# A turned strip's sixteen block moves: SyncE begins all of them, ScalarE none

## The chip, the cores and the metric

One core of one Trainium2 chip. The metric is the time of one launch on the device, in microseconds (us). TensorE (PE in the profile), VectorE (DVE), ScalarE (ACT), GpSimd (POOL) and SyncE (SP) each run their own list of instructions in order and meet at semaphores. SyncE computes nothing: it begins DMA transfers and waits.

## What is computed

One decoder layer over 256 tokens of width 2048 in float32. Cut to what matters here:

```python
h = rmsnorm(x, g_mix);  proj = h @ w_in                       # twelve parts: q, k, v, indexer, gates
out_a = dsa_sparse_attention(...);  out_b = forgetting_attention(...)
mixed = sigmoid(gate_a) * (out_a @ w_o_a) + sigmoid(gate_b) * (out_b @ w_o_b)
x = x + mixed @ w_out
h = rmsnorm(x, g_ffn)
x = x + (silu(h @ w_ffn_gate) * (h @ w_ffn_up)) @ w_ffn_down  # 5632 wide
h = rmsnorm(x, g_ple)
x = x + sigmoid(h @ w_ple_gate) * (p @ w_ple_proj)
return rmsnorm(x, g_final)
```

## The kernel before, in words

**Weights.** All weights stream from HBM in chunks of 512 KB (two tiles of 128 rows by 512 columns, in the stages that matter here). SyncE loads a chunk into one of four slots `ws` (`load`, L279). ScalarE copies it, rounded, into `hs` (`split_high`, L416), VectorE stores the rest `ws - hs` in `ls` (`split_low`, L720), and TensorE uses both (`by_token`: L1275 with `hs`, twice, for the high and low part of the activations; L1280 with `ls`). There are four slots of each. SyncE may load chunk c when VectorE has split chunk c-4 (`slot_free`); ScalarE may split chunk c when TensorE has used chunk c-4. A chunk waits for its high split before its first matmul and for its low split before its last four.

**Stages.** From the middle of the kernel on, results are made in strips of 512 columns. A "WO" stage (four of them) takes 8 chunks of `w_o_b` and `w_o_a` and makes one strip of `mixed`. An "OUT" stage (four) takes 8 chunks of `w_out` and makes one strip of x. An FFN pair (eleven; ten of them in a loop of two per pass) takes 8 chunks of the gate and 8 of the up weights and makes one strip of `ff`. A "DOWN" stage (four) takes 22 chunks, a "PLE" stage (four) takes 9. The stages follow each other without a gap in TensorE's list.

**Turning.** TensorE leaves a strip with tokens on the partitions, and the next product needs it with columns on the partitions. VectorE transposes 32x32 blocks of the strip into `t_rows` (`turn_quads`, L989, two instructions, semaphore `turned`). Sixteen DMAs inside SBUF, 32 KB each, then move block (a, q) to block (q, a) of `t_cols` (`move_quads`, L224, semaphore `moved`). Half of them, with q even, are begun by SyncE, the other half by ScalarE. When all sixteen have landed, ScalarE and VectorE write the high and the low part of the strip (`mixed_high` L570 and `mixed_low` L994; `new_high` L598 and `new_low` L1023; `ff_hi` L646 and `ff_low` L1090). 23 strips are turned: four of `mixed`, four of x after OUT, eleven of `ff`, four of x after DOWN.

**Order.** All lists are written out by hand. In SyncE's list the moves of the strip that the last stage made stand behind the loads of the first eight chunks of the running stage; the loads of the next chunks stand behind the moves. With the chunks of a stage called c0, c1, ..., the order is: load c0 to c7, wait for `turned`, begin 8 moves, load c8 (the c0 of the next stage where a stage has eight chunks), and so on. In ScalarE's list (`split_and_move`) the other 8 moves stand between the high splits of c5 and c6, and behind c7 stands the high part of the strip, then (WO stages) two sigmoids of the gates (L581), then the high splits of c8 to c11. VectorE's list is: low splits of c4 to c7, low part of the strip, low splits of c8 to c11, then the work on the finished strip (WO: three instructions from L1008 on; OUT and DOWN: L1030) and the turn.

Most stages use the turned strips of an earlier kind of stage and have long had them. Three strips are wanted at once: the fourth strip of `mixed`, by chunk c6 of the first OUT stage; the fourth strip of x, by c6 of the first FFN pair; the fourth strip of x after DOWN, by c7 of the first PLE stage.

Of the kernel before, what the change touches and what calls it, by code (L numbers as in the profile page):

```python
# [62 lines left out]
N_WIDE = D_MODEL // WIDE  # L63
N_FFN = D_FF // WIDE
C_WO, C_OUT, C_FFN = 4 * U_WO, 4 * U_OUT, 4 * U_FFN
# [8 lines left out]
QUADS = P // QUAD  # L74
# [38 lines left out]
def hybrid_layer(nc, c_rows, x, p, positions, g_mix, w_in, b_f, w_o_a, w_o_b, w_out, g_ffn, w_ffn_gate,  # L113
# [102 lines left out]

        return t.rearrange("p k (b a n) -> p (k b) a n", b=2, a=QUADS)

    def move_quads(eng, t, odd):

        eng.wait_ge(turned, 2 * t + 2)
        for a in range(QUADS):
            for q in range(odd, QUADS, 2):
                eng.dma_start(t_cols[QUAD * q:QUAD * (q + 1), a, :, :, :],  # L224
                              t_rows[QUAD * a:QUAD * (a + 1), q, :, :, :]).then_inc(moved, 16)

# [37 lines left out]
    @block.sync  # L264
    def _(sp):

        for b in range(2):
            sp.dma_start(x_tok[:, b, :], x_rows[:, b, :]).then_inc(x_loaded[b], 16)
        for n, g in enumerate((g_mix[0], g_ffn[0], g_ple[0])):
            sp.dma_start(gain_rows[n * KT:(n + 1) * KT, :], g.rearrange("(t q) -> t q", q=P)).then_inc(gains_loaded, 16)  # L270
        sp.dma_start(bias_f[F_ROWS, :], b_f[0].rearrange("(h o) -> h o", o=1)).then_inc(bias_loaded, 16)

        def slot_free(u, j):

            sp.wait_ge(l_split, 4 * (u - 1) + j + 1)

        def load(j, src, n=CHUNK):
            parts = src.shape[1]
            sp.dma_start(ws[:, j, 0:n].rearrange("p (t n) -> p t n", t=parts), src).then_inc(w_loaded[j], 16)  # L279


        sp.wait_ge(ring_zero, SLOTS)
        for j in range(SLOTS):
            slot = ws[:, j, 0:SMALL].rearrange("p (t n) -> p t n", t=KC)
            rows = win_t[:, KC * j:KC * j + KC, :]
            for at, col, n in ((0, AT_KI, D_IDX + H_IDX), (F_ROW, AT_FB, HB)):
                sp.dma_start(slot[:, :, at:at + n], rows[:, :, col:col + n]).then_inc(w_loaded[j], 16)

        def columns(u0, units, w, col0):

            with sp.Fori(0, units) as i:
                for j in range(SLOTS):
                    slot_free(u0 + i, j)
                    load(j, w[:, KC * j:KC * j + KC, ds(col0 + i * GROUP, GROUP)])

        columns(U_QI, 4, win_t, AT_QI)
        columns(U_QB, 8, win_t, AT_QB)

        def wide_columns(u0, units, w, col0):

            with sp.Fori(0, units) as i:
                for c in range(K_CH):
                    slot_free(u0 + c // SLOTS + i * (K_CH // SLOTS), c % SLOTS)
                    load(c % SLOTS, w[:, KW * c:KW * (c + 1), ds(col0 + i * WIDE, WIDE)])

        wide_columns(U_VB, 2, win_t, AT_VB)
        wide_columns(U_GA, N_WIDE, win_t, AT_GA)
        columns(U_QA, 6, win_t, AT_QA)
        wide_columns(U_GB, N_WIDE, win_t, AT_GB)
        for i in range(N_WIDE):  # L310
            for c in range(K_CH):
                slot_free(U_WO + c // SLOTS + i * 2, c % SLOTS)
                w, t = (wob_t, woa_t)[c // SLOTS], KW * (c % SLOTS)
                load(c % SLOTS, w[:, t:t + KW, WIDE * i:WIDE * (i + 1)])
            if i > 0:
                move_quads(sp, T_MIX + i - 1, 0)

        sp.wait_ge(o_ready, FREE + HEADS)
        sp.dma_start(p_tok[:, :, :], p_rows).then_inc(p_loaded, 16)
        for i in range(N_WIDE):  # L320
            for c in range(K_CH):
                slot_free(U_OUT + c // SLOTS + i * 2, c % SLOTS)
                load(c % SLOTS, wout_t[:, KW * c:KW * (c + 1), WIDE * i:WIDE * (i + 1)])
            move_quads(sp, T_MIX + N_WIDE - 1 + i, 0)
        with sp.Fori(0, N_FFN) as i:
            for half, w in enumerate((wgate_t, wup_t)):
                for c in range(K_CH):
                    slot_free(U_FFN + 2 * half + c // SLOTS + i * 4, c % SLOTS)
                    load(c % SLOTS, w[:, KW * c:KW * (c + 1), ds(i * WIDE, WIDE)])
                if half == 0:  # L330
                    move_quads(sp, T_FF - 1 + i, 0)
        for n in range(N_WIDE):
            for c in range(FF_CH):
                at = C_DOWN + FF_CH * n + c
                slot_free(at // SLOTS, at % SLOTS)
                load(at % SLOTS, wdown_t[:, KW * c:KW * (c + 1), WIDE * n:WIDE * (n + 1)])
                if c == K_CH - 1:
                    move_quads(sp, T_PLE - 1 + n, 0)
        for n in range(N_WIDE):
            cols = slice(WIDE * n, WIDE * (n + 1))  # L340
            for c in range(PLE_CH):
                at = C_PLE + PLE_CH * n + c
                slot_free(at // SLOTS, at % SLOTS)
                load(at % SLOTS, wpp_t[:, :, cols] if c == 0 else wpg_t[:, KW * (c - 1):KW * c, cols])
                if n == 0 and c == K_CH - 1:
                    move_quads(sp, T_PLE + N_WIDE - 1, 0)

        for n in range(2):
            cols = slice(D_MODEL // 2 * n, D_MODEL // 2 * (n + 1))
            sp.wait_ge(y_ready_0, 2 * n + 2)  # L350
            sp.dma_start(out_rows[:, 0, cols], out_tok[:, 0, cols]).then_inc(out_stored, 16)
        cols = slice(WIDE * 3, D_MODEL)
        sp.wait_ge(y_ready_0, 5)
        sp.dma_start(out_rows[:, 1, cols], out_tok[:, 1, cols]).then_inc(out_stored, 16)
        sp.wait_ge(out_stored, 4 * 16)
# [50 lines left out]
    def _(act):  # L406
# [152 lines left out]
            for at in range(first, first + n):  # L559
                split_high(at // SLOTS, at % SLOTS)  # L560

        def split_and_move(first, t):

            split_chunks(first, 2)
            move_quads(act, t, 1)
            split_chunks(first + 2, 2)

        def mixed_high(n):
            act.wait_ge(moved, 16 * MOVES * (T_MIX + n + 1))
# [3 lines left out]
        for n in range(N_WIDE):  # L573
            cols = slice(WIDE * n, WIDE * (n + 1))
            if n == 0:
                split_chunks(C_WO + 4, 4)
            else:
                split_and_move(C_WO + 8 * n + 4, T_MIX + n - 1)
                mixed_high(n - 1)
            for gate in (1, 0):  # L580
                act.activation(gates[:, gate, :, cols], gates[:, gate, :, cols], ACT.Sigmoid).then_inc(gate_ready, 1)  # L581
            split_chunks(C_WO + 8 * n + 8, 4)
# [20 lines left out]
            act.activation(rms[:, stage, 0, :], sum_sq[:, stage, :], ACT.Sqrt, bias=eps[:, 0:1], scale=1.0 / D_MODEL).then_inc(rms_sqrt, 1)  # L603

        for n in range(N_WIDE):
            split_and_move(C_OUT + 8 * n + 4, T_MIX + N_WIDE - 1 + n)
            if n == 0:
                mixed_high(N_WIDE - 1)
                act.wait_ge(p_t, 1)
                act.activation(p_cols[:, :, 0:TOK], side[:, 2, :].rearrange("p (m n) -> p m n", m=2), ACT.Copy).then_inc(p_high, 1)  # L610
            else:
                squares(0, n - 1)
                new_high(0, n - 1)
            split_chunks(C_OUT + 8 * n + 8, 4)

        def ff_pair(i, step, first=False):

            u = U_FFN + 4 * step + i * 8
            c = step + i * 2
            split_high(u + 1, 0)  # L620
            split_high(u + 1, 1)
            move_quads(act, T_FF - 1 + c, 1)
            split_high(u + 1, 2)
            split_high(u + 1, 3)
            if first:
                squares(0, 3)
                new_high(0, 3)
                root(0)
            else:
                ff_hi(c - 1)  # L630
            for j in range(SLOTS):
                split_high(u + 2, j)
            if first:
                act.wait_ge(rms_ready, 1)
            for b in range(2):
                ins = act.activation(silu_g[:, b, :], acc[:, 2 + b, :], ACT.Silu, scale=rms[:, 0, 1, b:b + 1])
            ins.then_inc(ff_silu, 1)
            for j in range(SLOTS):
                split_high(u + 3, j)
            for j in range(SLOTS):  # L640
                split_high(u + 4, j)
# [10 lines left out]

        for n in range(N_WIDE):
            at = C_DOWN + FF_CH * n
            split_and_move(at + 4, T_PLE - 1 + n)
            if n == 0:
                ff_hi(N_FFN - 1)
            else:
                squares(1, n - 1)
                new_high(1, n - 1)  # L660
            split_chunks(at + 8, FF_CH - 4)
# [5 lines left out]
        for n in range(N_WIDE):  # L667
# [1 line left out]
            if n > 0:  # L669
                split_chunks(at + 4, 4)  # L670
            if n == 0:
                split_and_move(at + 4, T_PLE + N_WIDE - 1)
                squares(1, 3)
                new_high(1, 3)
                act.dma_start(g_out[:, :], g_final.partition_broadcast(P)).then_inc(g_out_loaded, 16)
# [816 lines left out]
```

## Time and profile before

| | |
|---|---|
| median of 3 runs | 1491.15 us (1489.91 to 1491.16) |
| the profiled execution | 1490.77 us |
| its span, first to last instruction | 1489.0 us |
| TensorE matmuls busy | 1459.5 us (98%) |
| ScalarE, VectorE busy | 690.6 us (46%), 884.0 us (59%) |
| DMA engines | 61.8% of their time on SyncE's queue, 2.1% on ScalarE's |
| bytes moved | 290.91 MB |

The profiled execution took 1.8 us more than its span, which lies before the first and behind the last instruction. DMA-issuing instructions are not counted as busy; in a timeline they stand under SPq and ACTq, the sequencers' own rows. A row of a timeline gives start, duration from the first to the last instruction that it merges, engine, line, operation, output and input, and the count; in brackets stands how long the engine was idle before it and what ended that.

### The profile page before, as it was taken

How to read it: one execution, taken by the hardware profiler on the slowest of the kernel's cores; microseconds unless marked ns; L12 is line 12 of the kernel's file. 1: busy time of each engine (PE TensorE's matmuls, PEld its weight loads, DVE VectorE, ACT ScalarE, POOL GpSimd, SP SyncE). 2: the span in 40 equal slices, each digit the busy share in tenths (PEclk: the TensorE clock that was granted, in tenths of full speed). 3: DMA queues.
4: the chain of work that ended last, by engine and by line, in shares of the span. 5: the costliest groups of instructions: out<-in, count | busy, mean ns of one | idle time of the engine just before them, and what ended most of it. 6: DMA issues, size and time to landing. Idle time of an engine off the chain costs nothing.

```text
span 1489.0 us, 19456 instructions
## 1 busy us (share of the span) xinstructions
PE 1459.5 (98%) x6841; PEld 1222.0 (82%) x6841; DVE 884.0 (59%) x1066; ACT 690.6 (46%) x846; POOL 49.9 (3%) x80
## 2 busy tenths in 40 slices
PE   5999999999999999999999999999999999999996
PEld 5888888888888888887888888888888888888885
DVE  6966776667655576665555555455555455554654
ACT  5644445544444455445444444444444343443544
POOL 0021001100111000000000000000000000000000
PEclk9999999999999999999999999999999999999998
DMA  6666565556655577666666666766666766666663
GB/s 193 178 204 169 160 222 170 169 170 190 183 166 167 163 236 232 211 208 214 205 209 210 202 191 205 212 207 210 205 204 184 221 204 197 210 190 209 213 215 109
DMA packets 182574, 290.91 MB, mean 195 GB/s; under 512 B 18745, under 2 KB 67825, under 8 KB 182001
## 3 DMA queue, kind: packets, MB, share of 16 engines
q1 hardware_dynamic: 172944, 281.02, 61.8%
q10 hardware_dynamic: 9568, 9.07, 2.1%
q8 instruction: 39, 0.64, 0.2%
q14 instruction: 23, 0.18, 0.0%
HBM read 275.87 MB, written 2.11 MB: 187 GB/s over the span
## 4 chain that ended last, share of the span: by engine, by line
PE 94%; DVE 3%; DMA 1%; ACT 1%; ACTq 1%; issue 0%; DVEq 0%
PE acc L1275 50%; PE acc L1280 25%; PE acc L1165 8%; PE acc L1174 4%; PE side L1275 2%; PE side L1280 1%; DVE ls L720 1%; ACTq L224 1%; DMA rope_c<-in_rope_rows 1%; PE side L1321 0%; DVE hn L775 0%; PE side L1327 0%; DMA t_cols<-t_rows 0%; ACT hs L416 0%; PE side L1335 0%
## 5 line engine op out<-in xcount | busy, mean ns | idle before, releaser
L720 DVE TENSOR_TENSOR ls<-ws,hs 128x1024 fp32r<-128x1024 f32 (+1 forms) x520 | 629.9, 1224 | 535.7 <-ACT hs L416 531.3
L416 ACT ACTIVATE hs<-ws 128x1024 fp32r<-128x1024 f32 (+1 forms) x520 | 544.1, 1056 | 717.8 <-PE acc L1280 505.0
L1275 PE MATMUL acc<-hs,xg 128*128 128x512 f32 x1648 | 407.1, 389 | 1.1 <-DVE xg L1023 1.1
L1275 PEld LDWEIGHTS acc<-hs,xg 128*128 128x128 f32 x1648 | 309.3, 188 | 65.6 <-DVE xg L1023 1.5
L1280 PE MATMUL acc<-ls,xg 128*128 128x512 f32 x824 | 220.2, 389 | 0.0
L1280 PEld LDWEIGHTS acc<-ls,xg 128*128 128x128 f32 x824 | 154.7, 188 | 32.1
L1275 PE MATMUL acc<-hs,ff 128*128 128x512 f32 x704 | 173.8, 389 | 0.0
L1275 PE MATMUL acc<-hs,hn 128*128 128x512 f32 (+1 forms) x704 | 171.9, 387 | 0.0
L1275 PEld LDWEIGHTS acc<-hs,ff 128*128 128x128 f32 x704 | 132.2, 188 | 27.4
L1275 PEld LDWEIGHTS acc<-hs,hn 128*128 128x128 f32 x704 | 127.1, 188 | 24.2
L1165 PE MATMUL acc<-hn,hs 128*128 128x512 f32 x560 | 139.2, 393 | 0.0
L1165 PEld LDWEIGHTS acc<-hn,hs 128*128 128x128 f32 x560 | 101.5, 189 | 18.9
L1280 PE MATMUL acc<-ls,ff 128*128 128x512 f32 x352 | 94.1, 389 | 0.0
L1280 PE MATMUL acc<-ls,hn 128*128 128x512 f32 (+1 forms) x352 | 90.4, 380 | 0.0
L1174 PEld LDWEIGHTS acc<-hn,ls 128*128 128x128 f32 x560 | 74.3, 191 | 5.1 <-DVE hn L775 0.7
L1280 PEld LDWEIGHTS acc<-ls,ff 128*128 128x128 f32 x352 | 66.1, 188 | 13.7
L1174 PE MATMUL acc<-hn,ls 128*128 128x256 f32 x560 | 75.9, 283 | 0.5 <-DVE hn L775 0.5
L1280 PEld LDWEIGHTS acc<-ls,hn 128*128 128x128 f32 x352 | 64.2, 188 | 13.1
L1275 PE MATMUL acc<-hs,mixed 128*128 128x512 f32 x256 | 63.5, 390 | 0.5 <-DVE mixed L994 0.5
L1275 PEld LDWEIGHTS acc<-hs,mixed 128*128 128x128 f32 x256 | 47.9, 188 | 10.9 <-DVE mixed L994 1.0
L533 ACT ACTIVATE lg<-lg,neg_max 128x128 f32<-128x128 f32 (+1 forms) x32 | 14.3, 448 | 47.0 <-DVE neg_max L935 47.0
L1280 PE MATMUL acc<-ls,mixed 128*128 128x512 f32 x128 | 34.2, 389 | 0.0
(192 smaller groups left out, 815.2 us busy)
## 6 DMA issues: line engine op xcount, KB each, us to landing
ws<-in_w_in SPq DMA_DIRECT2D x152, 512.0 KB, 3.9
ws<-in_w_ffn_gate SPq DMA_DIRECT2D x88, 512.0 KB, 4.4
ws<-in_w_ffn_up SPq DMA_DIRECT2D x88, 512.0 KB, 4.4
ws<-in_w_ffn_down SPq DMA_DIRECT2D x88, 512.0 KB, 4.3
ws<-in_w_out SPq DMA_DIRECT2D x32, 512.0 KB, 4.7
ws<-in_w_ple_gate SPq DMA_DIRECT2D x32, 512.0 KB, 3.9
ws<-in_w_o_b SPq DMA_DIRECT2D x16, 512.0 KB, 4.6
ws<-in_w_o_a SPq DMA_DIRECT2D x16, 512.0 KB, 4.6
```

The lines of the kernel that those rows point to most:

```text
L224: eng.dma_start(t_cols[QUAD * q:QUAD * (q + 1), a, :, :, :], t_rows[QUAD * a:QUAD * (a + 1), q, :, :, :]).then_inc(moved, 16)
L416: act.activation(hs[:, j, 0:n], ws[:, j, 0:n], ACT.Copy).then_inc(h_split, 1)
L533: act.activation(lg[:, cols], lg[:, cols], ACT.Exp, bias=neg_max[:, b:b + 1], accum_out=sums[:, b:b + 1]).then_inc(exp_done, 1)
L720: dve.tensor_tensor(ls[:, j, 0:n], ws[:, j, 0:n], hs[:, j, 0:n].bitcast(F32), ALU.subtract).then_inc(l_split, 1)
L1165: mm = pe.matmul(acc_of(bank + m, 2 * TOK), hs[:, j, at], src[:, k, :], start=first and q == 0, stop=last and q == len(tiles) - 1)
L1174: mm = pe.matmul(acc_of(bank + m, TOK), ls[:, j, at], src[:, k, 0:TOK], start=False, stop=False)
L1275: pe.matmul(banks[b], block_of(src, k, part, b), hs[:, slot, q * width:(q + 1) * width], start=first and q == 0 and part == 0, stop=False)
L1280: mm = pe.matmul(banks[b], block_of(src, k, 0, b), ls[:, slot, q * width:(q + 1) * width], start=False, stop=last and q == len(tiles) - 1)
```

## The change

`move_quads` loses its argument `odd` and begins all sixteen moves of a strip. SyncE calls it where it called it before. ScalarE no longer calls it: `split_and_move` is gone, and four high splits stand in its place.

```diff
-    def move_quads(eng, t, odd):
+    def move_quads(eng, t):
 
         eng.wait_ge(turned, 2 * t + 2)
         for a in range(QUADS):
-            for q in range(odd, QUADS, 2):
+            for q in range(QUADS):
                 eng.dma_start(t_cols[QUAD * q:QUAD * (q + 1), a, :, :, :],
                               t_rows[QUAD * a:QUAD * (a + 1), q, :, :, :]).then_inc(moved, 16)
@@ SyncE, at all of its six call sites @@
-                move_quads(sp, T_MIX + i - 1, 0)
+                move_quads(sp, T_MIX + i - 1)
@@ ScalarE @@
-        def split_and_move(first, t):
-
-            split_chunks(first, 2)
-            move_quads(act, t, 1)
-            split_chunks(first + 2, 2)
@@
-                split_and_move(C_WO + 8 * n + 4, T_MIX + n - 1)
+                split_chunks(C_WO + 8 * n + 4, 4)
@@ and likewise for OUT, DOWN and the first PLE stage; in ff_pair @@
-            move_quads(act, T_FF - 1 + c, 1)
```

## Rows read from the trace of the kernel before

**Rows 1.** The page's busy times: busy us, share of the span, instructions.
```profile
PE 1459.5 (98%) x6841; PEld 1222.0 (82%) x6841; DVE 884.0 (59%) x1066; ACT 690.6 (46%) x846; POOL 49.9 (3%) x80
```
**Rows 2.** Waits of TensorE from 485 us on: us in total, times, longest.
```profile
PE acc L1275 <- DVE xg L1023: 1.1, 1, 1.1
PE acc L1275 <- DVE mixed L994: 0.5, 1, 0.5
```
**Rows 3.** Waits of SyncE's sequencer, whole span: us in total, times, longest.
```profile
SPq L279 <- DVE ls L720: 984.4, 470, 8.0
```
**Rows 4.** Timeline of the second WO stage, which begins at 505.79.
```profile
505.79 1.77 PEld L1275 LDWEIGHTS acc<-hs,heads_o 128*128 128x128 f32 x8
...
508.51 1.77 PEld L1275 LDWEIGHTS acc<-hs,heads_o 128*128 128x128 f32 x8
...
513.49 5.06 SPq L224 DMA_DIRECT2D t_cols<-t_rows  x8
513.49 5.38 ACTq L224 DMA_DIRECT2D t_cols<-t_rows  x8
...
518.59 4.24 SPq L279 DMA_DIRECT2D ws<-in_w_o_b  x4
518.98 2.01 ACT L416 ACTIVATE hs<-ws 128x1024 fp32r<-128x1024 f32 x2 [6.20 <-issue]
...
521.84 1.99 ACT L581 ACTIVATE gates<-gates 128x1024 f32<-128x1024 f32 x2
```
**Rows 5.** The moves, by tile: ns min/median/max, first and last start; then their landing.
```profile
L224 SPq DMA_DIRECT2D t_cols<-t_rows x184: 512/592/1624, 513.5 to 1388.6; - x184
...
DMA to landing us min/median/max: 1.8/1.9/4.5
```
**Rows 6.** Two loads begun back to back behind moves, by line L279, and each one's landing.
```profile
L279 SPq DMA_DIRECT2D ws<-in_w_o_b x1: 584/584/584, 518.6 to 518.6; - x1
DMA to landing us min/median/max: 4.6/4.6/4.6
...
L279 SPq DMA_DIRECT2D ws<-in_w_o_b x1: 482/482/482, 519.2 to 519.2; - x1
DMA to landing us min/median/max: 5.4/5.4/5.4
```
**Rows 7.** Timeline, end of that stage: merge of the next strip, and its moves.
```profile
530.89 1.22 DVE L1008 TENSOR_TENSOR mix_b<-acc,gates 128x1024 f32<-128x1024 f32 x1
...
535.87 4.97 SPq L224 DMA_DIRECT2D t_cols<-t_rows  x8
```
**Rows 8.** Timeline of the first OUT stage: the fourth strip of `mixed`.
```profile
578.77 4.97 SPq L224 DMA_DIRECT2D t_cols<-t_rows  x8
...
586.08 1.05 ACT L570 ACTIVATE mixed<-t_cols 128x1024 fp32r<-128x1024 f32 x1
...
588.81 1.69 PEld L1275 LDWEIGHTS acc<-hs,mixed 128*128 128x128 f32 x8 [0.97 <-DVE mixed L994]
```
**Rows 9.** Timeline of the second OUT stage: new x, and its moves.
```profile
596.89 1.22 DVE L1030 TENSOR_TENSOR x_tok<-acc,x_tok 128x1024 f32<-128x1024 f32 x1
...
599.47 4.96 SPq L224 DMA_DIRECT2D t_cols<-t_rows  x8
```
**Rows 10.** Timeline of the first FFN pair: the fourth strip of x.
```profile
664.75 5.83 SPq L224 DMA_DIRECT2D t_cols<-t_rows  x8
...
675.09 1.71 ACT L598 ACTIVATE xg<-t_cols,gains 128x256 fp32r<-128x256 f32 x4 [0.20 <-DMA t_cols<-t_rows]
...
677.23 2.11 PE L1275 MATMUL acc<-hs,xg 128*128 128x512 f32 x8 [1.07 <-DVE xg L1023]
```
**Rows 11.** SyncE's timeline of the second FFN pair.
```profile
709.82 5.16 SPq L224 DMA_DIRECT2D t_cols<-t_rows  x8
715.18 14.06 SPq L279 DMA_DIRECT2D ws<-in_w_ffn_up  x8
```
**Rows 12.** SyncE's timeline, second DOWN stage.
```profile
1204.68 5.97 SPq L224 DMA_DIRECT2D t_cols<-t_rows  x8
```

More of the change, by code:

```diff
@@ L323, in _ @@
                 load(c % SLOTS, wout_t[:, KW * c:KW * (c + 1), WIDE * i:WIDE * (i + 1)])
-            move_quads(sp, T_MIX + N_WIDE - 1 + i, 0)
+            move_quads(sp, T_MIX + N_WIDE - 1 + i)
         with sp.Fori(0, N_FFN) as i:
@@ L330, in _ @@
                 if half == 0:
-                    move_quads(sp, T_FF - 1 + i, 0)
+                    move_quads(sp, T_FF - 1 + i)
         for n in range(N_WIDE):
@@ L337, in _ @@
                 if c == K_CH - 1:
-                    move_quads(sp, T_PLE - 1 + n, 0)
+                    move_quads(sp, T_PLE - 1 + n)
         for n in range(N_WIDE):
@@ L345, in _ @@
                 if n == 0 and c == K_CH - 1:
-                    move_quads(sp, T_PLE + N_WIDE - 1, 0)
+                    move_quads(sp, T_PLE + N_WIDE - 1)
         for n in range(2):
@@ L605, in _ @@
         for n in range(N_WIDE):
-            split_and_move(C_OUT + 8 * n + 4, T_MIX + N_WIDE - 1 + n)
+            split_chunks(C_OUT + 8 * n + 4, 4)
             if n == 0:
@@ L654, in _ @@
             at = C_DOWN + FF_CH * n
-            split_and_move(at + 4, T_PLE - 1 + n)
+            split_chunks(at + 4, 4)
             if n == 0:
@@ L671, in _ @@
             if n == 0:
-                split_and_move(at + 4, T_PLE + N_WIDE - 1)
+                split_chunks(at + 4, 4)
                 squares(1, 3)
```

## The prediction

> **What bounds the kernel now.** I read the busy times first: TensorE's matmuls fill 1459.5 of 1489.0 us [rows 1]. Then the list of waits from 485 us on, where all the turning happens: TensorE waits twice, for the low part of the fourth `mixed` strip and of the fourth x strip [rows 2]. Everything else there is hidden behind matmuls, so there are at most some 2.3 us to win (worked out below), and the question is how much cover the moves have. SyncE's waits say where to look: it waits 984.4 us for free slots [rows 3]. That reads as an idle engine, but it is an average. Behind `turned` stands a list without such waits, and the timelines of single stages show its length.
>
> A chunk takes TensorE 508.51 - 505.79 = 2.72 us [rows 4], so a stage of eight takes 21.76 us. I write S for a stage's start, T for the start of SyncE's moves, M for the time from T to the next load, L for the start of that load.
>
> **Part 1: ScalarE loses its moves.** In the WO stage it issues for 5.38 us, and the splits of c6 and c7 come after an idle time of 6.20 us [rows 4]. Both are wanted by TensorE later than that anyway (TensorE does not wait there, [rows 2]), so removing 23 such stretches is worth nothing by itself. What could be gained is the two waits of TensorE.
>
> **Part 2: SyncE issues sixteen.** The eight moves and the step to the load take 518.59 - 513.49 = 5.10 us [rows 4]. A move takes 592 ns in the median and 512 at least, plus the step to the next [rows 5]; eight in 4.97 us are 0.63 apart [rows 8]. Eight more cost 8 x 0.63 = 5.0 us, so M goes from 5.1 to 10.1. The trace never shows SyncE issuing moves well away from ScalarE's. Bounds: 9.0 if alone each takes the shortest 512 ns plus 0.05 for the step, and 11.1 if one stretch of slow issue is met per strip, as in two of the stages (5.83 and 5.97 us for eight, [rows 10, 12]). I take 10.1, the row of most strips.
>
> The moves themselves are quick: 1.9 us to landing [rows 5]. The last of sixteen starts at T + 9.5 and lands at T + 11.4. In the x strips this costs little, because ScalarE's last moves used to land behind the next weight load: the high part began at 675.09 - 664.75 = T + 10.3 [rows 10].
>
> The Trainium skill (DMA: Bandwidth & Descriptors, section "Issuing engines are not separate DMA queues") says that issuing from several engines saves only the sequencers' time, "which is usually small relative to the DMA itself". Here eight issues take 5.0 us and one transfer 1.9, so I hold it not to be small; by the rule the sum below would be zero (the first rival).
>
> **Part 3: what is queued behind the moves on SyncE.** The load of c8. Its landing takes 4.6 us with another load right behind it [rows 6]; split and steps add 1.16 (1.06 for the instruction, about 0.05 before and behind it). So TensorE can have c8 at L + 5.8, and wants it at S + 21.76. Per kind of stage:
> - WO: T = S + 7.7 (513.49 - 505.79, [rows 4]). Before: 7.7 + 5.1 + 5.8 = 18.6, hidden. Now 7.7 + 10.1 + 5.8 = 23.6: late by **1.8**. ScalarE's own list is no later: strip at T + 11.4, its high part 1.05 [rows 8], two sigmoids 1.99 [rows 4] make T + 14.4, and c8 lands at T + 14.7.
> - OUT: T = S + 5.3 (L1030 one chunk after the stage's start, then 599.47 - 596.89 = 2.58, [rows 9]). 5.3 + 10.1 + 5.8 = 21.2: hidden by 0.6.
> - FFN pair: T is 5.45 after its start, and the step to the load is 715.18 - 709.82 = 5.36 [rows 11], so M = 10.4: 21.65, hidden by 0.1. Eight more chunks follow, in which the lists catch up.
> - DOWN: like OUT with eight moves of 5.97 [rows 12], M = 11.1: 22.2, late by 0.4, in three stages; 22 chunks let it catch up. The PLE strip goes like OUT and is hidden.
>
> **Part 4: late loads make the next strip late.** With c8 to c11 all waiting behind the moves, four loads go out together. Two begun 0.6 us apart land 1.4 us apart (518.6 + 4.6 and 519.2 + 5.4, [rows 6]), so c11 lands at L + 8.8 and its low split ends at L + 11.2. VectorE's merge of the finished strip stands behind that split. The trace shows this already: in the next stage the merge begins at 530.89 and T is 535.87, 4.98 later [rows 7], which is S + 8.3 and not 7.7. So from a WO stage T' = L + 11.2 + 4.95, and L' = T' + 10.1. Stage to stage that is 11.2 + 4.95 + 10.1 = 26.25 us against 21.76: **+4.5 for each further stage of this kind**, and T sits at S + 10.4. From an OUT stage it is 11.2 + 2.6 + 10.1 = 23.9: +2.1, T at S + 8.0.
>
> **The sum**, in order:
> - WO stages two to four: 1.8, 4.5, 5.1 (the last has the load of `p_tok`, 0.6, in the queue too): 11.4.
> - First OUT stage, fourth `mixed` strip. T = S + 10.4, strip landed + 11.4, low part complete 588.81 - 586.08 = 2.73 after the high part's start [rows 8]: S + 24.5. TensorE wants it at S + 6 x 2.72 + 0.55 for transposes in between = S + 16.9, so it waits 7.6, against 588.81 - 587.94 = 0.9 before: +6.7. This long wait lets the loads catch up.
> - OUT stages two to four: the second 0 with T = S + 5.3 (21.2), the third 1.5 (T = S + 7.4), the fourth 2.1: 3.6.
> - First FFN pair, fourth x strip: T = S + 8.0, landed + 11.4, first tiles + 2.14 (677.23 - 675.09, [rows 10]): S + 21.5. Wanted at S + 16.3: waits 5.2, against 1.45 before (the pair starts at 659.45, so wanted at 675.77): +3.8.
> - FFN 0; DOWN 3 x 0.4 = 1.2; PLE 0.
> Together 11.4 + 6.7 + 3.6 + 3.8 + 1.2 = 26.7 us. The span becomes 1515.7, the execution 1517.5. The profiled execution stood 0.4 under the median; I forecast **1517.5 us** (+1.8%).
>
> By the bounds of M alone: with 9.0 the same recurrence gives 0.7 + 3.4 + 4.0 + 5.6 + 0.3 + 2.7 = 16.7, so 1507.5. If loads in a burst land 1.95 and not 1.4 us apart, 37 us, 1528.
>
> **Rivals.**
> - *No change*, the case on the other side. The sequencers share what writes the descriptors, and a queue alone issues faster than beside another. For: issues take 512 ns at first and 592 in the median [rows 5]. Against: 512 is still a floor seen with a queue just begun. It decides at M of 6.9, 0.43 us a move: then T + M + 5.8 stays under 21.76 even with T at S + 9.0, and only the `mixed` strip costs about 1. Time 1491 to 1493. Chance 0.07. The skill's rule points here.
> - *Faster*: only the two waits of TensorE could go, 0.9 + 1.45 = 2.3 us, if in addition the strips landed sooner: 1489. Chance 0.02.
> - *Late loads but no feedback*: the four loads land early enough that T keeps its place. Then three WO stages 1.8 each and 0.6, the `mixed` strip 7.7 + 11.4 + 2.7 - 17.7 = 4.1, the x strip 5.3 + 11.4 + 2.1 - 17.8 = 1.0, DOWN 1.2: 12.3 us, 1503. Against it stands the 8.3 of [rows 7]. Chance 0.2.
> - *Slow issue in every strip*: M = 11.1, and the FFN pairs lose their cover, 5.45 + 11.4 + 5.8 - 21.76 = 0.9 in each of eleven. The recurrence gives 2.8 + 5.5 + 6.1 + 7.7 + 6.6 + 4.7 outside the FFN, 10 in it and 1.2 in DOWN: 44.6 us, 1535. Chance 0.14.
> - The forecast, with M between 9.0 and 10.5 and the spread of the burst: 1507 to 1528. Chance 0.57.
>
> **How the numbers follow.** The range leaves out no change and faster (0.09) and what lies above the slow issue; it reaches from under the case without feedback to the slow issue: 1500 to 1536. About 3 us (0.2%) is what a measurement of this kernel can tell from no change: slower 0.92, same 0.06, faster 0.02.
>
> **What would show it.** In the profile after: SyncE's rows of sixteen moves, with about 10.0 us from T to the last one's end (right for part 2 between 9.0 and 11); no ACTq row of L224, and splits of c6 and c7 on time; waits of TensorE's L1275 at the first chunk of WO stages on ScalarE's L416 and through it on DMA `ws`, of 1.8, 4.5 and 5.1 us; T at S + 10.4 in the third and fourth WO stage; a wait of over 7 us on L994 and over 5 on L1023; next to no waits between 720 and 1160 us. The prediction is wrong if SyncE's moves stand under 0.45 us apart, or if T keeps to S + 7.7 in WO stages. The FFN's cover of 0.1 us is the thinnest: if a landing there takes 5.0 instead of 4.6, eleven waits of 0.3 appear.

## The result and the profile after

The changed kernel takes **1522.16 us** (median; 1521.39 to 1525.15) against 1491.16: a ratio of 1.0214, 95% interval 1.0202 to 1.0226, or 31 us. I had forecast 1517.5 and slower. The profiled execution has a span of 1519.6 us, 30.6 more than before.

The page's busy times and its DMA queues (packets, MB, share of the 16 engines):

```profile
PE 1468.0 (97%) x6841; PEld 1226.7 (81%) x6841; DVE 888.1 (58%) x1066; ACT 696.4 (46%) x846; POOL 50.0 (3%) x80
...
q1 hardware_dynamic: 181776, 287.06, 61.3%
q10 hardware_dynamic: 736, 3.03, 0.5%
```

Against [rows 1], TensorE did the same 6841 matmuls in 8.5 us more busy time. The same bytes moved; ScalarE's queue (q10) has lost its moves to SyncE's (q1). So there is no more work anywhere, only a different order.

SyncE's timeline, which answers to [rows 4], [rows 7] and [rows 8]:

```profile
513.57 11.10 SPq L224 DMA_DIRECT2D t_cols<-t_rows  x16
524.71 2.12 SPq L279 DMA_DIRECT2D ws<-in_w_o_b  x4
...
540.50 10.02 SPq L224 DMA_DIRECT2D t_cols<-t_rows  x16
550.56 2.12 SPq L279 DMA_DIRECT2D ws<-in_w_o_b  x4
...
566.02 10.02 SPq L224 DMA_DIRECT2D t_cols<-t_rows  x16
...
593.89 10.01 SPq L224 DMA_DIRECT2D t_cols<-t_rows  x16
```

Sixteen moves take 10.0 us (11.1 the first time), and behind each of the first two blocks four weight loads go out at once, in 2.12 us. The first of them, begun at 524.71, lands in 4.6 us, as one did before [rows 6]: it is late because it is begun late, not because it is carried more slowly. The second block begins 10.0 us after its stage's start at 530.5, the third 10.0 after 556.0; before, these two blocks began 8.3 [rows 7] and 7.8 us (at 557.07) after their stages' starts.

What delayed the second block stands in VectorE's timeline:

```profile
530.41 5.19 DVE L714 TENSOR_TENSOR ls<-ws,hs 128x1024 fp32r<-128x1024 f32 x4 [2.16 <-ACT hs L416]
535.52 1.22 DVE L1002 TENSOR_TENSOR mix_b<-acc,gates 128x1024 f32<-128x1024 f32 x1
...
539.16 1.30 DVE L983 STREAM_TRANSPOSE t_rows<-mix_b 128x512 f32<-128x512 f32 x2
```

The low splits of the four late loads stand ahead of the merge (L1002, which was L1008). They end at 535.60, 10.9 us after L = 524.71, the merge follows at once, and the turn ends at 540.46, just ahead of the moves at 540.50.

All of TensorE's waits up to the second FFN pair, from its timeline (the bracket is the idle time and what ended it; the lines of TensorE and VectorE are 6 lower than before, L1269 for L1275, while L224, L279 and L416 have kept theirs):

```profile
530.52 2.06 PE L1269 MATMUL acc<-hs,heads_o 128*128 128x512 f32 x8 [2.50 <-ACT hs L416]
...
556.01 2.90 PE L1269 MATMUL acc<-hs,heads_o 128*128 128x512 f32 x8 [3.48 <-ACT hs L416]
...
582.66 2.08 PE L1269 MATMUL acc<-hs,mixed 128*128 128x512 f32 x8 [2.99 <-ACT hs L416]
607.53 3.78 PE L1269 MATMUL acc<-hs,mixed 128*128 128x512 f32 x8 [7.75 <-DVE mixed L988]
...
659.60 2.09 PE L1269 MATMUL acc<-hs,mixed 128*128 128x512 f32 x8 [0.91 <-ACT hs L416]
683.14 2.08 PE L1269 MATMUL acc<-hs,xg 128*128 128x512 f32 x8 [1.50 <-ACT hs L416]
...
704.73 3.78 PE L1269 MATMUL acc<-hs,xg 128*128 128x512 f32 x8 [4.98 <-DVE xg L1017]
```

Where [rows 2] had two waits there are seven, all ending between 530 and 705 us. Five are for a high split whose load was late, two for a strip. Note the second column: eight matmuls take 1.98 us in a running stage, 2.1 after most of the waits, but 2.90 and 3.78 after the longest. The windows say why (window; length, PE busy; granted clock; DMA share, GB/s):

```profile
558.00:560.00 2.00, 2.00 (x7) 0.50 0.94 250
...
607.50:609.50 2.00, 1.97 (x5) 0.50 1.05 405
609.50:611.50 2.00, 2.00 (x6) 0.50 0.97 374
...
613.50:615.50 2.00, 2.00 (x11) 1.00 0.83 294
```

The granted clock stood at 0.50, that is 1.2 instead of 2.4 GHz, for some 4 us of matmuls after TensorE had stood idle for 7.75 us, and came back to 1.00.

I count lateness from one chunk's start to the next, less 2.72 us, which is a little more than the idle time. Late chunks: 2.85, 3.84, 3.34, 8.12, 1.26, 1.85, 5.37, together 26.6, and 0.4 in one DOWN stage; less the 2.35 of before, 24.7. The chunks right behind three of the waits took 4.01, 4.53 and 4.86 us instead of 2.72, and two more were a little long: 6.0 us for the clock. Together 30.7 of 30.6 us.

### The profile page after: what moved, and what is told of

It reads as the page before. It is cut to its first block, busy times and chain, and to the rows that moved or that the text cites. A ratio compares the mean times of both kernels' runs of the same rounds, so it can differ in the third digit from the quotient of the medians.

```text
span 1519.6 us, 19446 instructions
## 1 busy us (share of the span) xinstructions
PE 1468.0 (97%) x6841; PEld 1226.7 (81%) x6841; DVE 888.1 (58%) x1066; ACT 696.4 (46%) x846; POOL 50.0 (3%) x80
## 3 DMA queue, kind: packets, MB, share of 16 engines
HBM read 275.87 MB, written 2.11 MB: 183 GB/s over the span
## 4 chain that ended last, share of the span: by engine, by line
PE 84%; SPq 6%; DVE 4%; DMA 4%; ACT 1%; issue 1%; DVEq 0%; ACTq 0%
PE acc L1269 45%; PE acc L1274 22%; PE acc L1159 8%; SPq L224 5%; PE acc L1168 4%; DMA ws<-in_w_out 1%; PE side L1269 1%; DMA ws<-in_w_o_b 1%; DVE ls L714 1%; DVE t_rows L983 1%; ACT hs L416 1%; DMA rope_c<-in_rope_rows 1%; SPq L279 1%; PE side L1274 0%; DMA ws<-in_w_ffn_gate 0%
## 5 line engine op out<-in xcount | busy, mean ns | idle before, releaser
L416 ACT ACTIVATE hs<-ws 128x1024 fp32r<-128x1024 f32 (+1 forms) x520 | 548.1, 1057 | 627.5 <-PE acc L1274 421.4
L1269 PE MATMUL acc<-hs,xg 128*128 128x512 f32 x1648 | 409.2, 391 | 6.5 <-DVE xg L1017 5.0
L1269 PEld LDWEIGHTS acc<-hs,xg 128*128 128x128 f32 x1648 | 310.6, 189 | 72.0 <-DVE xg L1017 5.4
L1269 PE MATMUL acc<-hs,ff 128*128 128x512 f32 x704 | 173.9, 389 | 0.0
L1269 PE MATMUL acc<-hs,hn 128*128 128x512 f32 (+1 forms) x704 | 171.9, 387 | 0.0
L1269 PEld LDWEIGHTS acc<-hs,ff 128*128 128x128 f32 x704 | 132.1, 188 | 27.8 <-issue 0.4
L1269 PEld LDWEIGHTS acc<-hs,hn 128*128 128x128 f32 x704 | 127.1, 188 | 24.2
L1269 PE MATMUL acc<-hs,mixed 128*128 128x512 f32 x256 | 65.4, 399 | 11.6 <-DVE mixed L988 7.7
L1269 PEld LDWEIGHTS acc<-hs,mixed 128*128 128x128 f32 x256 | 48.8, 192 | 23.0 <-DVE mixed L988 8.2
L1084 DVE TENSOR_TENSOR ff<-t_cols,ff 128x1024 f32 (+1 forms) x11 | 13.5, 1225 | 50.5 <-ACT ff L640 50.5
L1017 DVE SCALAR_TENSOR_TENSOR xg<-t_cols,gains,xg 128x128 fp32r<-128x128 f32 x64 | 17.5, 346 | 41.2 <-ACT xg L593 41.2
```

The lines of the kernel that those rows point to most:

```text
L416: act.activation(hs[:, j, 0:n], ws[:, j, 0:n], ACT.Copy).then_inc(h_split, 1)
L1017: ins = dve.scalar_tensor_tensor(in_quads(xg[:, 1, k:k + 1, :])[:, b], by_tile(t_cols)[:, 2 * m + b], gain, in_quads(xg[:, 0, k:k + 1, :]. ...
L1084: dve.tensor_tensor(in_quads(ff[:, 1, ds(c * 4, 4), :]), by_tile(t_cols), in_quads(ff[:, 0, ds(c * 4, 4), :].bitcast(F32)), ALU.subtract). ...
L1269: pe.matmul(banks[b], block_of(src, k, part, b), hs[:, slot, q * width:(q + 1) * width], start=first and q == 0 and part == 0, stop=False)
```

## The experiments

All times are medians, beside the kernel before on the same chip: 1490.58 us for the first four, 1490.77 for the next four, 1490.69 for the last four. Line numbers shift from kernel to kernel. In most, TensorE's product with `hs` stands at L1280 and the one with `ls` at L1285 (L1275 and L1280 before), the moves at L227, ScalarE's split at L421.

**Where does it cost? Only the FFN's eleven strips.**

```diff
 SyncE, in the FFN loop
-                    move_quads(sp, T_FF - 1 + i, 0)
+                    move_quads(sp, T_FF - 1 + i, 0, ALL)
 ScalarE, in ff_pair
-            move_quads(act, T_FF - 1 + c, 1)
+            move_quads(act, T_FF - 1 + c, 1, [])
```

> SyncE begins all sixteen moves of the eleven strips that are moved during FFN pairs (the fourth x strip and ten of ff); all other strips as before. By my theory the loads behind the moves still come in time there (turned 5.45 us after a pair's start, 10.4 to the load, 5.8 to the split: 21.65 of 21.76), so only the x strip costs: it is complete 1.0 us later than before. Expected +0.5 to +1.5 us, 1492. Rival, that each strip costs its share wherever it is (30.6 us / 23 = 1.3): 11 x 1.3 = +14.6 us, 1506. Rival, that the FFN's cover of 0.1 us is too thin: +3 to +5 us.

Measured 1493.33 us (ratio 1.002, 1.001 to 1.003): +2.8. The timeline of TensorE's weight loads shows the wait for the fourth x strip, and there is no other in the FFN:

```profile
678.56 2.38 PEld L1280 LDWEIGHTS acc<-hs,xg 128*128 128x128 f32 x8 [2.81 <-DVE xg L1028]
```

The ten strips of `ff` cost nothing; the cover of 0.1 us held. The x strip made its chunk 1.3 us later than before (2.77 against 1.45), and the chunk behind took 4.18 us, 1.5 too long, with the granted clock at 0.50. In this profiled execution half of the 3.0 us is the clock, for which I had allowed nothing. The ten executions fall into two groups, five from 1492.07 to 1492.91 (four of them within 0.1 us, +1.5, the upper end of my range) and five from 1493.75 to 1495.50. That the clock falls in the one group and not in the other would fit; only one execution was profiled, so it is not shown. A cost by share is refuted.

**Only the three strips of the WO stages.** Same edit at the WO call sites.

> SyncE begins all sixteen moves of the three strips moved during WO stages; the others as before. By my theory: first late load 1.8 to 2.9 us, then by feedback (the next strip is turned 10 us instead of 7.7 after its stage's start) 4 and 3.3, the fourth mixed strip is turned late too and its wait grows by 2 to 2.5, and one wait of over 3.4 us costs another 1.5 us at half the TensorE clock: +12 to +14 us, 1504. Rival without feedback: 3 x 1.8 + 0.6 = +6 us, 1497. Rival by share: 3 x 1.3 = +4 us.

Measured 1505.23 us (1.0104, 1.0087 to 1.012): +14.7, a little over my +12 to +14; its profiled span is 13.5 over. Late chunks of 3.0, 2.6 and 4.7 us, 2.3 for the mixed strip, and 3.0 of clock. I had expected 4 and then 3.3 us for the second and third: here the slow chunks came behind the first wait, the stage was longer by 1.5 us, and the second chunk was less late for it. Three strips of 23 make nearly half of the loss, and the rival without feedback (+6) is refuted.

**One strip only, the fourth of mixed.** The same edit for `i == 0` of the OUT loop.

> SyncE begins all sixteen moves of one strip only, the fourth strip of mixed, which TensorE wants at once. By my theory it is complete at S + 7.7 + 11.4 + 2.7 = S + 21.8 where TensorE wants it at S + 16.9: a wait of 4.5 to 4.9 us against 0.9 before, +4. After a wait of this length the granted clock should stand at half for some 3 to 4 us, as after the waits of 3.8, 8.1 and 5.4 us in the changed kernel, which costs 1.6 to 2.7 more: +5.6 to +6.5 us, 1497. Rival, that the clock has nothing to do with the wait: +4.0 us, 1495. Rival by share: +1.3.

Measured 1496.38 us (1.0045, 1.0029 to 1.0062), and 1495.96 in a second set: +5.3 to +5.8. The chunk was 5.04 us late and the next one took 4.52, 1.8 too long. The rival without the clock (+4.0) is refuted.

**ScalarE's relief alone.** SyncE's calls stay, ScalarE's are gone, `MOVES` is 8, and the consumers read `t_rows`. Half of the moves are left out, so the strips are not turned rightly; the time still bounds what ScalarE's relief can be worth.

> Part 1 alone, with work left out: SyncE begins its eight moves as before, ScalarE's eight are left out altogether and the consumers read the unmoved strip, so half of the moves' work is missing and the strips are not turned rightly. By my theory ScalarE's freed 5.3 us per strip are worth nothing but the two waits of TensorE of 0.9 and 1.45 us, which vanish since the strips are complete at T + 7: 1488.5 to 1489.5 us, -2.3. Rival, that ScalarE's issuing was a cost of its own: clearly under 1485 us.

Measured 1488.73 us (0.9989, 0.998 to 0.9999): -1.9. TensorE has no wait from 480 us on. The relief is worth no more than that, and it is the two waits of [rows 2].

**Half the dose.** `ALL[:12]` on SyncE, `ALL[12:]` on ScalarE, in every strip.

> Half the dose in all 23 strips: SyncE begins twelve moves, ScalarE four. M, the time from the turn to the next load, should be 7.6 us. By my theory 7.7 + 7.6 + 5.8 = 21.1 still hides in the first WO stage, and only the feedback of the late burst bites afterwards: waits of about 0.9, 2.2 and 4.3 us, nothing in OUT, FFN and DOWN: +6.7 us including the clock, 1497.5. Rival, that the cost is in proportion to the moves given to SyncE: half of 31 us, 1506.5. Rival of a threshold without feedback: no more than +2, 1493.

Measured 1500.04 us (1.0066, 1.0049 to 1.0083): +9.3, nearer to 1497.5 than to 1506.5, and not to 1493. This run sets the feedback apart from the late load itself. SyncE's timeline, then the start of two WO stages in TensorE's weight loads:

```profile
513.53 8.35 SPq L227 DMA_DIRECT2D t_cols<-t_rows  x12
...
537.45 7.49 SPq L227 DMA_DIRECT2D t_cols<-t_rows  x12
```
```profile
527.60 1.77 PEld L1280 LDWEIGHTS acc<-hs,heads_o 128*128 128x128 f32 x8
...
551.13 1.68 PEld L1280 LDWEIGHTS acc<-hs,heads_o 128*128 128x128 f32 x8 [1.82 <-issue]
```

The stage at 527.60 begins without any wait. But its four loads had gone out in a burst, from 521.93 on in 2.11 us, and the next moves begin at 537.45, 9.85 us after the stage's start instead of 8.3 [rows 7]. The stage after it is late by 1.8 although it has fewer us of moves in front of its load than the one that was on time. The next is late by 2.4.

**A load between the moves.** In the WO stages and the first three OUT stages: `ALL[:8]`, the next stage's first load, `ALL[8:]`.

> As the changed kernel, but in WO and OUT stages SyncE begins eight moves, then the next stage's first load, then the other eight. By my theory that load is only one of two paths that are nearly equally late: ScalarE's split of that chunk stands behind the strip's high part and two sigmoids and can't begin before T + 15. So WO stages still wait 2.1 to 3.6 us, the mixed strip 6.5, the x strip 4.8: 1513 to 1517, 5 to 9 us faster than the changed kernel. Rival, that this load's place in SyncE's queue is the whole matter: no waits in WO and OUT, only the two strips late: 1500 to 1502.

Measured 1518.41 us (1.0189, 1.0172 to 1.0206), 3.8 us below the changed kernel (3.4 when each is taken against its own kernel before): the theory's side, 1.4 us outside my numbers. The late chunks in WO are 2.2, 3.6 and 2.0 us, so the place of this one load is not the whole matter. With the load in time, ScalarE's own list is the later path: at the first of them the strip's high part begins at 525.85, two sigmoids follow, and the split of the stage's first chunk comes only at 528.71, without any wait for its load. My error was in the strips, the mixed one above all: 8.5 us late where I had 6.5, its moves beginning 10.9 us after the stage's start. I did not follow that up.

**The mirror image.** `[]` on SyncE, `ALL` on ScalarE, everywhere.

> The mirror image: ScalarE begins all sixteen moves, SyncE none. SyncE's loads are then never late and there is no feedback, but the high splits of c6 and c7 stand behind ten us of issuing: by my theory waits of 2.6 us in each of three WO stages, about 0.8 in every other stage that turns a strip, 5 to 6 for the two strips wanted at once and 3 for the third: +36 to +42 us, 1528 to 1533. Rival, that it is all the same which queue begins the moves: 1522. Rival, that only a late weight load hurts: under 1500.

Measured 1541.13 us (1.0342, 1.0325 to 1.0359): +50. Right in kind, not in size. From ScalarE's timeline of an OUT stage:

```profile
619.46 11.46 ACTq L227 DMA_DIRECT2D t_cols<-t_rows  x16
631.02 2.01 ACT L421 ACTIVATE hs<-ws 128x1024 fp32r<-128x1024 f32 x2 [10.53 <-PE acc L1285]
```

The splits of c6 and c7 stand behind the moves as expected, but the block took 11.5 us here and not 10.1, and the chunk was 2.3 us late where I had 0.8; the FFN pairs were late by 1.0 each and not 0.8. Net of the waits of before, late chunks make some 43 of the 50 us and slow chunks behind them some 7, a term that I had left out. ScalarE is the worse of the two for this, since it has a split due in every stage.

**The merge earlier.** In the changed kernel, VectorE's WO stage:

```diff
-            split_chunks(C_WO + 8 * n + 8, 4)
+            split_chunks(C_WO + 8 * n + 8, 2)
             ...
             turn_quads(mix_b, 0)
+            split_chunks(C_WO + 8 * n + 10, 2)
```

> As the changed kernel, but in WO stages VectorE merges and turns the finished strip behind the low split of c9 instead of c11. It tests the feedback (a late burst of loads delays the next turn). By my theory T in the third and fourth WO stage moves from S + 10 to S + 7.5, the waits for the late first load there fall from 3.8 and 3.3 to about 1.5 with some 1.4 new for the low split of c10, and the mixed strip's wait falls from 8.1 to about 5.5: 3 to 6 us faster than the changed kernel, 1516 to 1519. Rival without feedback, that each load is late by its sixteen moves alone: T and the first waits unchanged, and the new waits add to them: 1522 or more.

Measured 1521.46 us (1.0207, 1.019 to 1.0224): no gain that can be told. T did not move. The mixed strip's wait did fall, to 6.0 us from 7.75, but the strip was not ready any earlier, 25.3 us after its stage's start against 24.9 in the changed kernel. TensorE had been held 2.1 us in the same stage, by a low split of the burst's third chunk, which now stood behind the merge; there is one more such wait, of 1.3 us, in the stage before. These I had expected, at some 1.4. The timeline of the third WO stage, which begins at 530.86:

```profile
532.04 8.83 SPq L279 DMA_DIRECT2D ws<-in_w_o_a  x4
...
536.93 1.31 DVE L983 STREAM_TRANSPOSE t_rows<-mix_b 128x512 f32<-128x512 f32 x2
...
540.91 10.02 SPq L224 DMA_DIRECT2D t_cols<-t_rows  x16
```

The strip was turned by 538.2, but SyncE began the moves only at 540.91. It was still in the loads before them. The list of SyncE's waits from 531 to 542 us, first of the changed kernel, then of this one:

```profile
SPq L279 <- DVE ls L714: 7.6, 4, 4.8
SPq L224 <- DVE t_rows L983: 4.5, 1, 4.5
```
```profile
SPq L279 <- DVE ls L714: 11.9, 4, 5.6
```

In the changed kernel SyncE stands 4.5 us before its moves and waits for the turn. Here it waits for low splits instead: the loads ahead of the moves need the splits of the burst's last two chunks, and I had put these behind the merge. So this edit took 4.5 us of waiting off one path and put them onto another. It shows that T has two conditions, the turn and the loads that SyncE has ahead of the moves. It does not show that the second would hold T by itself: in the changed kernel these loads are out by 535.99 (531.66 + 4.33), 4.5 us ahead of T. Nor does it refute the feedback. A kernel in which the merge comes early and those splits are not delayed was not tried, so that the late burst holds T rests on the order of VectorE's rows in the changed kernel and on the half dose, and no run has taken it away.

**Is the clock a consequence of the idle time?** The kernel with one late strip again, and the same with 19 matmuls ahead of the wait:

```diff
+                if n == 0 and c == 6:
+                    for _ in range(19):
+                        pe.matmul(side[:, 3, :], mixed[:, 0, 0, 0:P],
+                                  mixed[:, 0, 0:2, :].rearrange("p k n -> p (k n)"), start=True, stop=True)
                 if n == 0:
                     pe.wait_ge(mix_ready, c // 2 + 1)
```

> The kernel of e3_mix3_only once more, as the partner of the next run: 1496.4 us.

> The kernel of e3_mix3_only, but ahead of its wait for the fourth mixed strip TensorE runs 19 matmuls of 512 columns into an unused bank, whose results nobody reads: about 19 x 0.227 = 4.3 us in a wait of 5.0. If the granted clock falls because TensorE stood idle, it stays at full speed here and the 1.8 us after the wait go away: 1494.3 to 1495 us. Rival, that the fall has another cause (the strip's transfers, the burst of loads, which are the same here): 1496.4, as without them.

Measured 1495.96 and 1493.57 us: **2.4 us faster with more work**, where I had expected 1.4 to 2.1 below the partner's 1496.4. Windows of the first, then of the second:

```profile
588.00:592.50 4.50, 0.21 (x1) 0.88 0.51 108
592.50:594.50 2.00, 1.53 (x4) 0.50 1.00 380
594.50:596.50 2.00, 2.00 (x6) 0.50 1.04 394
```
```profile
588.00:592.50 4.50, 4.50 (x20) 1.00 0.47 115
592.50:594.50 2.00, 1.55 (x8) 1.00 1.03 387
594.50:596.50 2.00, 2.00 (x11) 1.00 1.05 403
```

The chunk starts at 592.97 and 592.95: the strip is equally late, and the transfers are nearly the same (380 and 387 GB/s in the first window behind the wait). Only the clock differs, and with it the chunk behind the wait (4.86 against 2.64 us). The Trainium skill (TensorE: Matmul & The Clock Gate, Part 1, section "What's actually happening") says that activity releases the throttle and idleness brings it back; these two runs agree.

**Can another division beat the kernel before?** First SyncE nine and ScalarE seven, `ALL[:9]` and `ALL[9:]`:

> The other way from the changed kernel, as little as possible: SyncE nine moves, ScalarE seven. SyncE's next load goes out 0.6 us later and ScalarE's last move 0.6 us earlier, so that the x strips' last moves no longer land behind a weight load. Expected: TensorE's wait of 1.45 us for the fourth x strip vanishes, the one for mixed stays, no load is late (7.7 + 5.7 + 5.8 = 19.2): 1489.3 to 1490 us, -1.4. Rival, that the landing is set by something else: 1490.8.

Measured 1490.06 us (0.9995, 0.9985 to 1.0004). The timeline at the fourth x strip:

```profile
665.32 6.31 SPq L227 DMA_DIRECT2D t_cols<-t_rows  x9
665.97 4.73 ACTq L227 DMA_DIRECT2D t_cols<-t_rows  x7
...
673.94 1.69 ACT L603 ACTIVATE xg<-t_cols,gains 128x256 fp32r<-128x256 f32 x4
```

The strip is used 8.6 us after T, not 10.3 [rows 10], and that wait is gone; the mixed strip's, which I had expected to stay, rose from 0.9 to 1.45. What remains of the 1.4 us that I had expected, 0.6, can't be told from no change.

Then three queues: SyncE six, ScalarE five, GpSimd five, with a semaphore of its own on which ScalarE also waits.

> SyncE begins six moves, ScalarE five, GpSimd (idle by then) five, with a semaphore of its own. If GpSimd issues as fast as the others, both waits of TensorE (0.9 and 1.45 us) vanish: 1488.5 to 1489.3 us, -1.9. Rival: GpSimd's issue or landing is slower and the strips come later than before: 1491 to 1500 us.

Measured **1488.82 us** (0.9986, 0.9977 to 0.9995), the fastest kernel that does all of the work, and TensorE has no wait from 480 us on. Issues by queue:

```profile
L227 SPq DMA_DIRECT2D t_cols<-t_rows x138: 512/592/1665, 513.5 to 1385.4; - x138
L227 ACTq DMA_DIRECT2D t_cols<-t_rows x115: 514/616/1419, 513.5 to 1385.1; - x115
L227 POOL DMA_DIRECT2D t_cols<-t_rows x115: 496/498/638, 513.7 to 1384.2; - x115
```

It beats both kernels, by 0.13% the one before. Spreading the issuing wider was the direction in which there was something to win; as no wait of TensorE is left in these stages, more could not be won there by moving the issuing about.

## Why the prediction was right, and where not

- **Part 1, ScalarE's relief is worth nothing by itself.** Right: the run without its moves gains only the two waits.
- **Part 2, M = 10.1.** Right: 10.06 in the third WO stage (550.56 - 540.50), so issuing alone is no faster on SyncE than beside ScalarE. The bound of 9.0 and the first rival fall. In six of the 23 strips a slow issue adds 0.3 to 1.2 us. Four of these are moved in DOWN stages, where I had counted on it; I had not at the first WO strip (1.1) or at one OUT strip (0.7). The 1.1 is why the first late load was 2.85 us and not 1.8.
- **Part 3, per kind of stage.** Right: nothing in the FFN, next to nothing in DOWN (0.4 and not 1.2) and PLE. The rule of the Trainium skill that issuing time is usually small beside the transfer (DMA: Bandwidth & Descriptors, section "Issuing engines are not separate DMA queues") does not hold for these transfers: one takes 0.63 us to issue and 1.8 to land, and the landings overlap while the issues do not, so sixteen take 10.0 us of issuing.
- **Part 4, the feedback.** Right in kind and nearly in size: T stood at S + 10.0 (forecast 10.4), the later WO stages were late by 3.84 and 3.34 (4.5 and 5.1), the mixed strip by 8.1 (7.6), OUT stages by 1.3 and 1.85 (1.5 and 2.1), the x strip by 5.4 (5.2). The stage before the 3.34 was itself 1.55 us longer, by the clock, so less of the lateness was left. From the late burst to the moves it took 15.8 us (524.71 to 540.50), where I had 11.2 + 4.95. Half the dose shows the next T late although no chunk of its stage was. That SyncE's own loads ahead of the moves are a second condition of T I had missed; in the changed kernel they had 4.5 us to spare. Two points were weaker than they looked. The S + 8.3 of [rows 7] is no good evidence for the feedback: in the next stage of the same trace the loads behind the moves went out half a microsecond later in their stage (540.88, against 518.59), and T came back to S + 7.8 (557.07); the burst of [rows 7] landed more slowly, its last load in 6.2 us. And in the first OUT stage T stood at S + 11.2 and not 10.4: `p_tok`'s load goes out ahead of the burst, and the burst's last load took 8.4 us to land, where the stage before took 6.6. The path from T to the low part was 0.5 us shorter than I had it, so that 8.1 came out near 7.6 in part by luck.
- **The sum.** My waits came to 26.7 us net, measured were 24.7. What is missing is a term that the sum did not have: the **clock**, 6.0 us. All my prices were for a TensorE at full clock, as [rows 2] were, since before the change nothing stopped it for long. With it the forecast would have been 1523.5. So 1517.5 lies as near as it does because two errors work against each other, waits 2.0 us too long and the clock at nothing; the range held both.
- **Rivals.** "No feedback" (1503) is refuted by T at S + 10, by the three WO strips alone (+14.7 against its +6) and by the half dose. "Slow issue in every strip" (1535) is not what happened, but in six strips it was.

## What to carry to other kernels

An in-order queue that also feeds the bound engine has a deadline per stage: add up what stands ahead of each load (here turn + issue + landing + split against the stage's length) before putting anything more on it, and look at the stage with the least room, not at the queue's mean idleness. If the sum goes over, expect more than the overshoot: loads that were held up go out together, the last of them delays what comes next, and a stage can't recover unless it is long enough. And price a new wait of the matmul engine with the slow chunk behind it.

## What was not expected of the hardware

- The granted clock fell to 0.50 after waits much shorter than I would have feared. In these traces chunks late by 3.5 us or more were always followed by slow matmuls, costing 1.4 to 2.7 us, unless the wait was filled. Between 2.3 and 3.5 us it went either way: 2.85 and 3.34 in the changed kernel without, 2.77 in the FFN-only kernel and 2.39 at half the dose with 1.5 us. Below that it did not happen in any of them. What decides between them is open.
- A move's issue takes 592 ns on SyncE's queue, alone or beside another (medians), and 498 on GpSimd's; single ones take up to 1.76 us (the first block lost 1.1 us to slow ones), and before the change both queues had them at once (1.42 us on SyncE's and 1.45 on ScalarE's, from 666 us on). The cause is open.
